# First modulation chunks summed in three pieces, with the first strip's units between them

## The reference, cut to what matters

```python
cond = jax.nn.silu(c)
mod = cond @ w_mod[l] + b_mod[l]
sh1, sc1, g1, sh2, sc2, g2, sh3, sc3, g3 = jnp.split(mod, 9, axis=-1)
h = modulate(x, norm_g[l, 0], sh1, sc1)     # rms norm, times gain and 1 + sc1, plus sh1
x = x + 0.5 * g1[:, None, :] * swiglu(h, w_ffn1_gu[l], w_ffn1_down[l])
...
bias = rel_table[t5_bucket(rel)]            # window attention's bias, made in the opening too
```

## Time and profile before

| | |
|---|---|
| median of three runs | 1761.39 us (1760.89 to 1761.67) |
| span of the profiled execution | 1759.8 us |
| what lies around the span (median less span) | 1.6 us |
| PE busy | 1732.4 us, 98% |
| DVE busy | 1419.2 us, 81% |
| ACT busy | 1006.7 us, 57% |
| HBM read | 438.38 MB, 250 GB/s over the span |

### The profile page before, as it was taken

The page is one execution under the profiler, slowest core; times in us unless marked ns, Lnnn a source line. Parts: engine busy times, 40 slices in busy tenths (PEclk is TensorE's granted clock), DMA queues, the critical chain, the costliest instruction groups (busy, mean ns, idle before and its releaser), DMA issues.

```text
span 1759.8 us, 24720 instructions
## 1 busy us (share of the span) xinstructions
PE 1732.4 (98%) x9178; PEld 1470.0 (84%) x9178; DVE 1419.2 (81%) x2185; ACT 1006.7 (57%) x1666; POOL 184.0 (10%) x382
## 2 busy tenths in 40 slices
PE   6999999999999999999999999999999999999998
PEld 3888888888888888988888888888888888888886
DVE  7899987898899888878888866579888876688565
ACT  5445577755475556877545644556455544465454
POOL 3021012111111111021110000001110000010000
PEclk9999999999999999999999999999999999999999
DMA  9999742699869985418898654459886483466551
GB/s 352 356 360 393 273 147 83 259 332 337 315 225 340 332 314 205 168 51 317 329 334 291 224 206 158 161 191 333 324 325 249 169 301 146 185 229 245 204 194 70
DMA packets 125144, 441.10 MB, mean 251 GB/s; under 512 B 15248, under 2 KB 18272, under 8 KB 124896
## 3 DMA queue, kind: packets, MB, share of 16 engines
q1 hardware_dynamic: 91024, 316.17, 49.1%
q0 software_dynamic: 33296, 120.12, 18.2%
q10 hardware_dynamic: 704, 3.23, 0.5%
HBM read 438.38 MB, written 1.09 MB: 250 GB/s over the span
## 4 chain that ended last, share of the span: by engine, by line
PE 94%; DVE 2%; DMA 2%; ACT 1%; issue 1%; SPq 0%; DVEq 0%; ACTq 0%
PE banks L2368 24%; PE banks L2169 15%; PE banks L2373 12%; PE banks L2147 11%; PE banks L2174 7%; PE banks L2152 6%; PE banks L2317 2%; PE banks L2321 2%; PE banks L2326 2%; PE banks L2137 1%; PE banks L2139 1%; PE banks L2138 1%; DMA weights_raw<-in_w_mod_first 1%; PE banks L2281 1%; DVE weights_lo L1355 1%
## 5 line engine op out<-in xcount | busy, mean ns | idle before, releaser
L1355 DVE TENSOR_TENSOR weights_lo<-weights_raw,weights_hi 128x1024 fp32r<-128x1024 f32 (+2 forms) x584 | 685.9, 1200 | 67.5 <-ACT weights_hi L810 66.7
L810 ACT ACTIVATE weights_hi<-weights_raw 128x1024 fp32r<-128x1024 f32 (+2 forms) x584 | 584.8, 1036 | 68.3 <-PE banks L2174 21.9
L2368 PE MATMUL banks<-hT,weights_hi 128*128 128x512 f32 x1856 | 464.1, 392 | 0.0
L2368 PEld LDWEIGHTS banks<-hT,weights_hi 128*128 128x128 f32 x1856 | 337.3, 189 | 63.0
L2373 PEld LDWEIGHTS banks<-hT,weights_lo 128*128 128x128 f32 x1856 | 253.2, 190 | 18.1
L1368 DVE CUSTOM_DVE_ANT_0 arena<-arena,mod_acc,vectors 128x1024 f32<-128x1024 f32 x216 | 267.6, 1280 | 0.0
L2373 PE MATMUL banks<-hT,weights_lo 128*128 128x256 f32 x1856 | 258.8, 282 | 0.0
L1004 ACT ACTIVATE arena<-banks 128x512 f32<-128x512 f32 x116 | 69.3, 598 | 323.1 <-PE banks L2373 322.9
L2147 PE MATMUL banks<-weights_hi,hT 128*128 128x512 f32 (+2 forms) x896 | 218.2, 385 | 0.0
L2147 PEld LDWEIGHTS banks<-weights_hi,hT 128*128 128x128 f32 x896 | 165.6, 188 | 29.9
L1690 DVE TENSOR_TENSOR arena<-banks,arena 128x512 f32<-128x512 f32 x116 | 79.8, 688 | 108.9 <-ACT arena L1004 108.9
(11 more groups left out here) (358 smaller groups left out, 1971.3 us busy)
## 6 DMA issues: line engine op xcount, KB each, us to landing
weights_raw<-in_w_ffn_gu SPq DMA_DIRECT2D x176, 512.0 KB, 4.5
arena<-in_w_mod POOLq DMA_DIRECT2D x128, 512.0 KB, 6.2
weights_raw<-in_w_in SPq DMA_DIRECT2D x104, 512.0 KB, 4.1
weights_raw<-in_w_ffn_down SPq DMA_DIRECT2D x88, 512.0 KB, 5.0
arena<-in_w_ada POOLq DMA_DIRECT2D x88, 512.0 KB, 5.6
weights_raw<-in_w_ffn_in SPq DMA_DIRECT2D x88, 512.0 KB, 4.1
weights_raw<-in_w_ffn_out SPq DMA_DIRECT2D x44, 512.0 KB, 4.5
weights_raw<-in_w_out SPq DMA_DIRECT2D x32, 512.0 KB, 3.8
```

Source lines behind the costliest of these rows:

```text
L810: nc.scalar.activation(whi[:, n % PARTS, 0:width], raw[:, slot, 0:width], ACT.Copy).then_inc(S("hi_done"), credit(n))
L1355: V.tensor_tensor(wlo[:, n % PARTS, 0:width], raw[:, n % RING, 0:width], whi[:, n % PARTS, 0:width].bitcast(F32), ALU.subtract).then_inc(S ...
L2368: T.matmul(half_banks(j)[:, kind, :], whi[:, n % PARTS, 256 * k + P * kind:256 * k + P * (kind + 1)], hx[:, :, 4 * q + k, :], start=q == 0 ...
```

## The change

The sixteen modulation units are laid out anew, and summed in three pieces (MOD_PIECES) instead of two chunks. The first piece, eight units, holds the scale and the shift of column blocks 0 to 3, the second (four units) blocks 4 and 5, the third (four units) blocks 6 and 7. Each piece has its own PSUM bank and its own piece_store on DVE, which also makes the scale. Column blocks 2u and 2u + 1 are what weight unit 6 + u of the first strip needs, so that unit's products (opening_high, opening_low) stand behind the piece that they need, between the later modulation units. SP loads units 6 to 9 between the modulation units, at the places that this needs, and then the second strip ahead of the constants and the gain rows. ACT takes over most of x_scaled in the opening and DVE's scaling of the normed x. The bias passes move: 0 to 2 lie between the first modulation units, 3 in the first strip, 4 and 5 in the second strip, with 5 at its very end; each takes three reductions instead of four. keep_warm, eight products with zeros that filled PE's wait before the first strip, goes.

```diff
+MOD_PIECES = ((0, 8, 0, 4), (8, 4, 4, 2), (12, 4, 6, 2))
+PIECE_BANKS = (3, 4, 5)
+REACHED_HOME = (0, 1, 2, 3, 2, 3)
+BIAS_BANKS = ((5, 6, 7), (0, 1, 7))
...
-            for m in range(MOD_FIRST_UNITS):
+            def first_weight(u):
+
+                slot = (RING + u) % RING
+                sp.dma_start(raw[:, slot, :], phases[0][2]["gu"][0, u]).then_inc(S(f"first_mod_loaded{FIRST_RING + slot}"), 16)
+
+            for m in range(0, 10):
                 mod_load(sp, m)
-            sp.wait_ge(S("mod_read"), 6)
-            gu_strip(RING, phases[0][2]["gu"], 0, (0,))
+            sp.wait_ge(S("mod_read"), reads_to(5))
+            first_weight(0)
+            first_weight(1)
+            for m in range(10, 12):
+                mod_load(sp, m)
+            sp.wait_ge(S("mod_read"), reads_to(6))
+            first_weight(2)
+            for m in range(12, 16):
+                mod_load(sp, m)
             sp.wait_ge(S("mod_summed"), 1)
-            gu_strip(RING, phases[0][2]["gu"], 0, (1,))
+            first_weight(3)
             for kind, n0, a in phases:
                 if kind == "ffn":
                     if n0 == RING:
-                        sp.wait_ge(S("mod_summed"), 2)
+                        sp.wait_ge(S("mod_summed"), len(MOD_PIECES))
+                        gu_strip(n0 + 4, a["gu"], 1)
                         sp.dma_start(con[:, C_MASKW:], A["con"][:, C_MASKW:]).then_inc(S("const_loaded"), 16)
...
-                        gu_strip(c, a["gu"], b)
+                        if n0 > RING or b > 1:
+                            gu_strip(c, a["gu"], b)
...
@@ -949,25 +979,27 @@
 
                 act.wait_ge(S("const_loaded"), 16)
                 nc.scalar.activation(table_col[:, :], ident[:, 0:1], ACT.Silu)
-                hi_static(RING, SLOT)
-                act.wait_ge(S("scale_ready"), 1)
-                act.wait_ge(S("mod_stored"), 2)
-                x_scaled(a, 0, True, (1,))
+                act.wait_ge(S("mod_stored"), 1)
+                x_scaled(a, 0, True)
                 x_hi(0)
                 x_scaled(a, 1, True)
                 x_hi(1)
-                act.wait_ge(S("mod_stored"), 3)
+                hi_static(RING, SLOT)
+                x_scaled(a, 2, True)
+                x_hi(2)
+                x_scaled(a, 3, True)
+                x_hi(3)
                 hi_static(RING + 1, SLOT)
-                x_hi(2)
-                x_hi(3)
-                hi_static(RING + 2, SLOT)
+                act.wait_ge(S("mod_stored"), 2)
                 x_scaled(a, 4, True)
                 x_hi(4)
+                x_scaled(a, 5, True)
+                x_hi(5)
+                hi_static(RING + 2, SLOT)
                 hi_static(RING + 3, SLOT)
-                x_hi(5)
+                act.wait_ge(S("scale_ready"), 1)
                 x_scaled(a, 6, True)
                 x_hi(6)
-                x_scaled(a, 7, True)
                 x_hi(7)
                 x_split_done()
...
+            def piece_store(i, a):
+
+                _, _, k0, blocks = MOD_PIECES[i]
+                dve.wait_ge(S("mod_summed"), i + 1)
+                eye = con[:, C_EYE:C_EYE + 32].unsqueeze(1).broadcast_to([P, 2 * blocks, 32])
+                sums = bank[PIECE_BANKS[i]][:, 0:64 * blocks].rearrange("p (k j) -> p k j", j=32)
+                cols = [w[:, 0:16].rearrange("p (c k) -> p c k", c=2)[:, :, k0:k0 + blocks] for w in (modc, vec)]
+                then(V.tensor_tensor(modm[:, 0:2 * blocks, :], sums, eye, ALU.mult))
+                then(V.tensor_reduce(modr[:, 0:2 * blocks], modm[:, 0:2 * blocks, :], AX, ALU.add))
+                then(V.tensor_tensor(cols[0], modr[:, 0:2 * blocks].rearrange("p (c k) -> p c k", c=2), cols[1], ALU.add))
+                last = i == len(MOD_PIECES) - 1
+                V.scalar_tensor_tensor(sclA[:, k0:k0 + blocks], modc[:, 8 + k0:8 + k0 + blocks], 1.0, vec[:, a["g"] + k0:a["g"] + k0 + blocks],
+                                       ALU.add, ALU.mult).then_inc(S("scale_ready" if last else "mod_stored"), 1)
...
             def bias_take(q):
 
                 dve.wait_ge(S("bias_summed"), q + 1)
-                for g in range(4):
-                    c = P * (q // 2) + 64 * (q % 2) + 16 * g
-                    ins = V.tensor_reduce(bias[:, :, c:c + 16], bank[g + (4 if q < 4 else 0)][:, 0:288].rearrange("p (k q h) -> p h k q", q=3, h=WH), AX, ALU.add)
+                for g in range(3):
+                    c, n = P * (q // 2) + 64 * (q % 2) + 24 * g, (24, 24, 16)[g]
+                    ins = V.tensor_reduce(bias[:, :, c:c + n], bank[BIAS_BANKS[q // 3][g]][:, 0:18 * n].rearrange("p (k q h) -> p h k q", q=3, h=WH), AX, ALU.add)
                 ins.then_inc(S("bias_taken"), 1)
...
             bias_reach(1)
-            dve.wait_ge(S("const_loaded"), 16)
+            x_stats(1, 0)
             bias_take(0)
             bias_reach(2)
+            x_stats(1, 1)
             bias_take(1)
-            x_stats(1, 0)
-            x_scale0(1)
-            bias_reach(3)
-            bias_take(2)
-            x_stats(1, 1)
-            x_scale1(1)
-            mod_store(1)
-            scale_cols(phases[0][2])
-            bias_take(3)
-            bias_reach(4)
-            mod_store(0, 0, 2)
+            dve.wait_ge(S("const_loaded"), 16)
             phase = [0]
             ffn_n, mid1_n, mid2_n = [0], [0], [0]
             for kind, n0, a in phases:
                 phase[0] += 1
                 if phase[0] == 1:
-                    dve.wait_ge(S("mod_stored"), 2)
-                    x_scaled(a, 0, (0,), first=True)
-                    mod_store(0, 2, 8)
-                    dve.wait_ge(S("mod_stored"), 3)
+                    scales[0] += 1
+                    piece_store(0, a)
+                    bias_take(2)
                     x_low(0)
+                    x_low(1)
                     lo_static(n0, SLOT)
-                    x_scaled(a, 2, first=True)
-                    x_low(1)
-                    x_scaled(a, 3, first=True)
-                    lo_static(n0 + 1, SLOT)
                     x_low(2)
                     x_low(3)
+                    piece_store(1, a)
+                    lo_static(n0 + 1, SLOT)
+                    bias_reach(3)
+                    x_low(4)
+                    x_low(5)
                     lo_static(n0 + 2, SLOT)
-                    x_low(4)
-                    x_scaled(a, 5, first=True)
-                    lo_static(n0 + 3, SLOT)
-                    x_low(5)
+                    dve.wait_ge(S("mod_stored"), 2)
+                    piece_store(2, a)
+                    dve.wait_ge(S("scale_ready"), 1)
+                    x_scaled(a, 7, first=True)
                     x_low(6)
                     x_low(7)
+                    lo_static(n0 + 3, SLOT)
                     x_split_done()
...
-                    units(n0 + 4, n0 + (8 if FIRST_TURNED[f] == 1 else 6))
                     if f == 0:
-                        bias_reach(5)
+                        units(n0 + 4, n0 + 5)
+                        bias_take(3)
+                        units(n0 + 5, n0 + 6)
+                        bias_reach(4)
+                    else:
+                        units(n0 + 4, n0 + (8 if FIRST_TURNED[f] == 1 else 6))
                     gated(0)
                     if f in loads_cond:
                         dve.wait_ge(S("cond_row_ready"), loads_cond.index(f) + 1)
                     for b in range(1, FIRST_TURNED[f]):
                         c = n0 + 4 + 6 * (b - 1)
-                        units(c + 2, c + 4)
-                        mod_units(mod_slot(f, b))
+                        units(c + 2, c + 3)
                         if f == 0 and b == 1:
                             bias_take(4)
+                            bias_reach(5)
+                        units(c + 3, c + 4)
+                        mod_units(mod_slot(f, b))
...
             def mod_unit(m):
 
-                chunk, k = m // 8, m % 8
+                i = piece_of(m)
+                first, units, _, blocks = MOD_PIECES[i]
+                each = KD // units
                 mod_wait(pe, m)
-                parts = mod_tile(m).rearrange("p (k r j) -> p r k j", r=4, j=32)
-                for r in range(4):
-                    ins = T.matmul(bank[sum_bank(chunk)][32 * r:32 * (r + 1), 0:256], silc[:, k:k + 1].broadcast_to([P, 32]), parts[:, r],
-                                   start=k == 0, stop=k == 7)
-                ins.then_inc(S("mod_summed" if k == 7 else "mod_read"), 1)
+                parts = mod_tile(m).rearrange("p (c k r j) -> p c r k j", c=each, r=4, j=32)
+                for c in range(each):
+                    k = each * (m - first) + c
+                    for r in range(4):
+                        ins = T.matmul(bank[PIECE_BANKS[i]][32 * r:32 * (r + 1), 0:64 * blocks], silc[:, k:k + 1].broadcast_to([P, 32]), parts[:, c, r],
+                                       start=k == 0, stop=k == KD - 1)
```

(56 more changed lines are left out.)

127 lines of the change are left out of this document (60 added, 67 removed).

## The result

| | before | changed |
|---|---|---|
| median of four runs | 1761.53 us (1760.89 to 1763.03) | 1771.7 us (1771.15 to 1772.4) |
| ratio, 95% interval | 1 | 1.0057, 1.0044 to 1.0069 |
| span of the profiled execution | 1759.8 us | 1770.1 us |
| mean granted clock | 0.999 | 0.995 |

The kernel is 10.2 us slower; 3.2 us were forecast, and 1767.5 us was the upper end of the range.

A forecast was written before the change was run, and what follows sets the result against it. TensorE, busy 98%, was the bound, with everything behind the first down products (58.48 us) moving together. The opening's 5.2 us gain was swallowed by unit 15's late landing, start 61.65: 1761.4 + 3.2 = 1764.6 us, range 1759.5 to 1767.5.

The forecast's parts named there:

- Rival 4: Opening on PE: sum units take 1.0 us, m15 is read at 36.7, total 1766.8 us; chance 0.09.
- rivals 2 and 3: At the down products: DVE decides, start 57.1, 1760.0 us, chance 0.13; or PE alone, 54.4, 1757.3 us, chance 0.08.
- Rival 1: Gain loads before the down pair take turns with POOL's packets: 7.3 us, unit 15 lands at 59.9, 1766.7 us; chance 0.30.
- gains take 5.2: On SP's queue between constants and down pair, the five gain loads take 5.2 us, the middle of 3.1 and 7.3.
- almost alone: On SP's queue behind the gain rows, the down pair follows with little beside it in 2.5 us, landing at 57.8.
- The tail "3.85 us": From unit 15's landing to the first down products: high part 1.05, low part 1.22, bias take 1.45, handing over 0.13.
- DVE's list: VectorE's work behind the first strip, 17.4 us from 39.7, ending at 57.1, before the down products.
- priced at that level: All PE products were priced at the full granted clock, 1.00 (2.4 GHz).
- cost nothing: The dropped keep_warm products lay in PE's wait for ACT, 29.99 to 32.59, so dropping them saves nothing.
- The block: Everything behind the first down products (58.48 us) moves as a whole; PE's later waits change by at most a microsecond.

The follow-up runs named there:

- The table of four versions: Changed kernel (1771.7 us), and it with gain rows moved to the first attention phase (1765.92), POOL's modulation loads behind unit 13's split (1764.35), or both (1763.43).
- the version with both later loads: Changed kernel with gain rows moved to the first attention phase and POOL's six modulation loads held until unit 13 is split: 1763.43 us, ratio 1.0015.
- its variant: Kernel before with only the five gain loads moved to the first attention phase: 1761.77 us, ratio 0.9999.

## Why the prediction was wrong

**Right:** the unit m15 is read by PE at 33.4 to 34.0 (34.5 forecast, 33.8 the floor), a sum unit is 0.64 with sixteen matmuls too, the strip ends near 40 and the next begins 4.7 us sooner (5.2), SP issues unit 10 at 34.10 (34.5), the take is 1.48 (1.45), and the landing of unit 15 decides, with window_bias named at PE's wait. Rival 4 fell with the sum units, rivals 2 and 3 with the landing. Rival 1 came nearest: its landing, 59.9, is 1.1 us short of the measured one.

**The term "gains take 5.2" failed.** From the constants' landing to the last gain row's it was 10.0 us (48.8 to 58.8). Rival 1's price, 7.3, is the rows by themselves (4.0) and POOL's remaining bytes on top (3.3); 5.2 is the middle, in which half of those bytes fit between the small packets. The table of four versions shows that none of them do: the rows cost the pair 4.0 us beside POOL's loads and 3.9 without, so the two costs add up, as in rival 1. The argument that the engines were "only 57% and 32% busy, so there is room" was wrong. Rival 1 was still too low, as POOL had more left at 48.8 than the 1.36 MB of the forecast (it moved 1.76 MB behind that), and the pair did not follow "almost alone" in 2.5 us: its packets ran beside the last rows and the packets of unit 16, which landed before unit 15. For the rows and the pair together 7.7 us were forecast and 12.2 measured. The constants landed 1.3 us sooner than forecast (48.8 against 50.1), so unit 15 was 3.2 us late against 57.8. The rows' own 4.0 was right by luck: the stretch that it was read from holds 0.38 MB, the five rows 0.17. What the Trainium skill's page DMA: Bandwidth & Descriptors (section Queues, rings and completion order), quoted for rival 1, says of taking turns by packet agrees with the even counts (436 and 432), and rival 1 deserved more than 0.30.

**The tail "3.85 us" failed** by 1.1. It counted unit 15 alone; ACT and DVE have both units of the pair to cut, since both wait for the pair's one semaphore. With a semaphore each the tail measured 3.84. The same slip stands in DVE's list: it was to start at 39.7, with unit 10's high half, but units 10 and 11 share a semaphore as well, and it started at 40.74. Here the late pair hid that; in the version with both later loads it shows as 57.8 against 57.1.

**The clock, "priced at that level", failed** by 2.1. A start 3 us later was priced, but not what a wait of 10.95 us does to PE's clock: 0.51 while it waits, 0.50 for the first 4 us of work behind it. The same may hold of the sentence that the dropped keep_warm products "cost nothing". In the profiled executions of two versions without zeros in the opening the first eight products took 3.65 us instead of 2.08, at a granted clock of 0.50:

```profile
23.46 3.65 PE L2320 MATMUL banks<-weights_hi,hT 128*128 128x512 f32 x8 [1.59 <-issue]
...
23.50:26.50 3.00, 3.00 (x7) 2.40 (x8) 1.96 (x3) 2.94 (x7) 0.00 (x0) 0.50 1.02 406
```

In six other such profiles, the changed kernel's among them, it stayed at 1.00, and it did in all four with zeros. That is too few to call it shown.

**The block held,** with the two ends as exceptions: the waits of PE behind 80 us are those of the earlier trace rows (0.8 us the longest, as before), the shift is 9.56 us at 74 us and 9.46 at 1750. The premise left out that the span ends with POOL, whose last DRAIN was 0.5 us longer.

Sum of what was mis-sized: 3.2 (landing: rows and pair 4.5 late, constants 1.3 soon) + 1.1 (tail) + 2.1 (clock) + 0.5 (end) = 6.9 us, against 10.2 - 3.2 = 7.0.

## What to carry to other kernels

A small broadcast load costs far more than its bytes: here five rows of 0.17 MB in all, directly ahead of the pair, cost it 4 us, with or without another queue beside them. Put them behind any load that decides the end, and add the other queue's bytes in full. Look which loads share a semaphore. Price a wait of TensorE with the clock that it loses, and cover one that cannot be removed with products of zeros, few enough to end before the wait does. And where an opening is sped up, look first at what the next load was waiting behind: here 4.7 us won on TensorE were worth nothing until two groups of loads and one reduction had been put elsewhere.

## What the hardware showed that was not expected

- **Small against large packets.** Even counts of packets, as above: 0.10 MB against 1.58 MB in 6 us. The same five rows took 3.9 us alone and 10.0 beside POOL's loads, but cost the pair behind them 4 us either way.
- **The lower clock outlasts the wait.** Behind 10.95 us of waiting, the first three groups of four products took 2.04, 1.91 and 1.51 us (1.07 to 1.20 at the full clock). Behind 2.6 us of waiting it was lost in the profiles of three versions (eight products slow in the one with POOL's loads later, start 57.75) and kept in one (start 57.91).
- **The last addition on POOL.** The profile of the kernel before, then of the changed one:

```profile
1750.23 1.29 POOL L792 TENSOR_TENSOR x<-x,arena 128x512 f32<-128x512 f32 x1 [113.44 <-DVE arena L1513]
...
1750.43 1.64 DVE L1539 TENSOR_TENSOR arena<-x,arena 128x512 f32<-128x512 f32 x1
```

```profile
1759.97 0.67 DVE L1575 TENSOR_TENSOR arena<-x,arena 128x512 f32<-128x512 f32 x1
1759.99 1.78 POOL L817 TENSOR_TENSOR x<-x,arena 128x512 f32<-128x512 f32 x1 [111.29 <-DVE arena L1549]
```

The same two additions meet in both kernels. Before, POOL's starts 0.20 us ahead and takes 1.29, and DVE's lasts 1.64; now DVE's starts 0.02 us ahead and takes 0.67, and POOL's lasts 1.78. Whoever starts first keeps its pace. All fourteen profiles agree: in the two of the kernel before and its variant POOL is first and the DRAIN takes 9.43 us, in the twelve of the changed kernel and its versions DVE is first and it takes 9.91 to 9.92. The Trainium skill's page SBUF — State Buffer (section SBUF: two separate sides) says that such a pair of DVE and GpSimd instructions competes for one exclusive port pair, given to the one that starts first; the four durations agree. The DRAIN that ends the span is longer by as much as POOL's addition (0.49 us), which suggests that it waits for it. No run tried it by itself.
